# A hybrid decoder step on one Trainium2 core: the places of the gate products in the RWKV recurrence

## The chip, the core and the metric

The kernel runs on one core of one Trainium2 chip. The metric is the device time of one execution in microseconds (us). The core has a matrix engine (TensorE, PE in the rows; its weight loads are PEld), VectorE (DVE), ScalarE (ACT), GpSimd (POOL) and SyncE (SP), which here issues most DMAs. The engines run their own instruction streams and meet by semaphores.

## What is computed

One decoder layer is applied to 256 prompt tokens and 32 sample tokens (8 sequences of 4). Cut to what matters here:

```
P  = rmsnorm(x) @ w_in                    # 1024 -> HGRN2 | RWKV-7 | gate_a, gate_b (2 x 1024 columns)
o_a = hgrn2_chunked(...)                  # branch A
S   = S*diag(w) - (S kk)(kk*a)^T + v k^T  # branch B, RWKV-7, token by token
y   = S r ;  o_b = groupnorm(y)*... * g
merged = sigmoid(gate_a) * (o_a @ w_branch_a) + sigmoid(gate_b) * (o_b @ w_branch_b)
x = x + merged @ w_out
x = x + moe_top4of32(rmsnorm(x)) ; final rmsnorm
```

The 2048 gate columns are wanted only when the branches are merged. They depend on nothing of the recurrence.

## The kernel before

**The recurrence in passes.** RWKV-7 on the prompt is done in chunks of 32 tokens. The loop `for u in range(4)` at L872 makes four passes; a pass handles 128 tokens (four chunks) of four heads. In a pass TensorE works through small products in a fixed order, which VectorE and ScalarE answer from PSUM:

- `chunk_scores` and `scores` (L896, L905), then `level(0)` (L941, L944), the first of five levels that invert the 32x32 triangular parts by repeated squaring;
- `to_rows(At, Bn)` (transposes, L924), site L0, `level(1)`;
- `to_rows(Kn, vR)`, site L1, `level(2)`;
- `key_scores` (L912), site L2, then the key product Y1 (L980). It waits for the third rise of `rw_T_evac`, which ScalarE makes when it has copied the key rows (`knT`, L1733) after the two copies of level 2 (`power_evac(2)`);
- `level(3)`, site L3, `level(4)`, site L4, `solve` (L957), the sums of the earlier pass's output (L869), site W, the products L993 to L1005, the second sums, site Y;
- the chunk products (L1016 to L1020) with a site after each head, k0 to k3. VectorE turns their result into `phi`, one operation for each chunk (L2240). From the second pass on, four transposes (L1029) follow k3;
- the chain over the four chunks: L1040 and L1049, then a site (c0 to c3). Chunk c's L1040 waits for `phi` of chunk c and for the state that VectorE made of chunk c-1 (L2248).

**The sites.** At a site `fill(u, site)` (L669) issues so many gate products: one is a matmul of a 128x128 weight block with 288 token columns in float32, which the trace shows as two MATMUL records (L660). Eight products sum one block of 128 gate columns in one of two PSUM banks; there are 16 blocks. The first 56 products stand before the passes, 18 stand in each pass. How many stand at a site is the table `FILL` (L378), written by hand:

```python
FILL = (("L0", 1), ("L1", 1), ("L2", 1), ("L3", 1), ("L4", 2), ("W", 2), ("Y", 2), ("k0", 0), ("k1", 0), ("k2", 0), ("k3", 1),
        ("c0", 2), ("c1", 1), ("c2", 1), ("c3", 3))
```

`gate_products` (L383) sums the table up to a site. ScalarE's `gate_evacs` (L1686) reads the same sum: at a site at which it passes a multiple of eight, ScalarE takes the finished block out of PSUM by an Exp (L1606). Site W of ScalarE's stream stands before `ob_square`, whose result the second sums (L869) need; in the first pass two DMA issues (L1636) stand before it too.

After the passes come the branch products (L1072), the merge, `w_out` (L1098), the router, and the experts (L1304, L1325 and others). The experts' weights stream from HBM into eleven places, each refilled when TensorE has used it.

Of the kernel before, what the change touches and what calls it, by code (L numbers as in the profile page):

```python
# [76 lines left out]
def layer_kernel(nc, x_prompt, x_sample, state_hgrn, state_rwkv, state_shift, norm1_w, w_in, hgrn_lb_logits,  # L77
# [5 lines left out]
    with ctx:  # L83
# [288 lines left out]
        def pj_after(n):  # L372
# [2 lines left out]

        E_BLOCK = 31
        WHOLE = 7
        FILL = (("L0", 1), ("L1", 1), ("L2", 1), ("L3", 1), ("L4", 2), ("W", 2), ("Y", 2), ("k0", 0), ("k1", 0), ("k2", 0), ("k3", 1),  # L378
                ("c0", 2), ("c1", 1), ("c2", 1), ("c3", 3))
        GATED = (0, 2, 1)  # L380
        FILL_U = sum(n for _, n in FILL)

        def gate_products(u, site):  # L383

            x = [name for name, _ in FILL].index(site)
            return KT * WHOLE + u * FILL_U + sum(n for _, n in FILL[:x + 1])

# [2291 lines left out]
```

How the kernel before makes its waits and increments, by code:

```python
        def done_wait(eng, ins, name):  # L257
            eng.wait_ge(S(name), done(ins, name))
# [12 lines left out]
        def half_wait(turn, s):  # L272
            if turn is None and (s == SPLIT or s - FULL in HALVED):
                nc.tensor.wait_ge(S("half_loaded"), 16 * (1 if s == SPLIT else HALVED.index(s - FULL) + 2))
# [55 lines left out]
        def pe_w_wait(turn, s):  # L331
            if turn is None:
                nc.tensor.wait_ge(w_loaded[place(s)], 16 * loads_into(place(s), s + 1))
            else:
                n = PEELED + s
                per_turn = QUAD * ECH // WS
                nc.tensor.wait_ge(w_loaded[place(n)], turn * (16 * per_turn) + 16 * (loads_into(place(n), n + 1) - TURN * per_turn))
# [56 lines left out]
        @block.sync  # L395
        def _(sp):
            sp.dma_start(norm_bc[0:1, :], norm1_w).then_inc(S("norm_loaded"), 16)
            for t, (o, n) in enumerate(TILES):
                src = x_prompt[0, o:o + n, :] if t < 2 else x_sample.rearrange("b t d -> (b t) d")
                sp.dma_start(xs[0:n, t, :], src).then_inc(S(f"x_loaded{t}"), 16)
            sp.dma_start(xn[NS:NS + NB, 2, :], state_shift[0]).then_inc(S("shift_loaded"), 16)
            for n in list(range(N_IN + 2)) + [N_IN + 6, N_IN + 7] + list(range(N_IN + 2, N_IN + 6)):
                if N_IN - 1 <= n < N_IN + 3:
                    sp.wait_ge(S("rw_W"), 2 * (n - N_IN + 2))
                if n == N_IN + 6:
                    sp.wait_ge(S("rws_out"), 16 * NB)
                if n == N_IN + 4:
```

## Time and profile before

| | us |
|---|---|
| median of 3 runs | 1298.42 |
| the runs | 1297.34 to 1302.24 |
| the profiled execution | 1299.21 |
| its span, first to last instruction | 1297.5 |
| TensorE busy | 1264.7 (97%) |
| the four passes, in the span | 206.3 to 311.4 |
| the experts' stage, in the span | about 392 to the end |

Times of rows are from the start of the span. Matmuls overlap in the array and their ends are modelled, so what a group of them costs is read from its start to the start of the next group. A semaphore's wait shows as the idle time in brackets at the end of a row only where nothing modelled covers it; the distance of two starts shows it always.

### The profile page before, as it was taken

The numbers are of one execution on the slowest core, as the hardware profiler recorded it, in microseconds if no ns is written. First come the engines' busy times: TensorE is split into PE (matmuls) and PEld (weight loads), VectorE is DVE, ScalarE is ACT, GpSimd is POOL, SyncE is SP. The second block draws the span as 40 slices with busy tenths as digits, with TensorE's granted clock in tenths as the row PEclk, the third lists the DMA queues.
The fourth block names the chain that finished last, engine by engine and source line by source line (L and its number), as shares of the span: only waits on it lengthen the run. The fifth ranks groups of instructions, "written<-read, shape, count | busy, mean of one in ns | idle before, by whom it ended". The sixth has DMA issues, their size and how long they took to land.

```text
span 1297.5 us, 20685 instructions
## 1 busy us (share of the span) xinstructions
PE 1264.7 (97%) x8541; PEld 588.6 (45%) x8541; DVE 362.1 (28%) x1012; ACT 239.4 (18%) x544; POOL 55.1 (4%) x120
## 2 busy tenths in 40 slices
PE   8999999999999999999999999999999999999997
PEld 6768767777653333333333333333333323233333
DVE  2334766443346112112121121112121111211112
ACT  3144343232032011101111111011110101110102
POOL 5000300000060000000000000000000000000000
PEclk9999999999999999999999999999999999999999
DMA  7645424423989999999999999999999999999996
GB/s 221 163 130 194 131 67 129 144 101 117 372 297 377 426 429 429 428 428 428 429 429 429 428 429 430 430 429 429 430 431 430 429 430 429 430 430 430 429 429 260
DMA packets 73261, 449.55 MB, mean 346 GB/s; under 512 B 14408, under 2 KB 43130, under 8 KB 47884
## 3 DMA queue, kind: packets, MB, share of 16 engines
q1 hardware_dynamic: 67462, 445.45, 84.1%
q10 hardware_dynamic: 5734, 3.14, 0.9%
q8 instruction: 51, 0.84, 0.3%
q14 instruction: 14, 0.11, 0.0%
HBM read 443.82 MB, written 4.76 MB: 346 GB/s over the span
## 4 chain that ended last, share of the span: by engine, by line
PE 78%; DMA 16%; DVE 3%; ACT 2%; issue 1%; ACTq 0%; SPq 0%; DVEq 0%
PE bank L1304 26%; PE bank L1325 14%; DMA arena<-in_expert_w_gu_dram 7%; DMA ring<-in_expert_w_gu_dram 7%; PE bank L570 7%; PE bank L1219 5%; PE bank L660 5%; PE bank L1250 5%; PE bank L1072 2%; ACT arena L1449 2%; PE bank L1226 1%; PE bank L1294 1%; DMA arena<-in_norm_w_dram 1%; PE bank L617 1%; PE bank L1315 1%; PE bank L941 1%
## 5 line engine op out<-in xcount | busy, mean ns | idle before, releaser
L1304 PE MATMUL bank<-ring,arena 128*64 128x512 f32 x1040 | 233.6, 594 | 5.0 <-DMA ring<-in_expert_w_gu_dram 5.0
L1449 ACT ACTIVATE arena<-bank 128x512 f32<-128x512 f32 (+6 forms) x237 | 117.5, 511 | 451.5 <-PE bank L1325 196.2
L1304 PE MATMUL bank<-arena 128*64 128x512 f32 x768 | 173.3, 594 | 2.4 <-DMA arena<-in_expert_w_gu_dram 2.4
L1449 ACT ACTIVATE arena<-arena 128x256 f32<-128x256 f32 (+7 forms) x124 | 68.8, 564 | 471.9 <-DVE arena L2430 463.6
L1304 PEld LDWEIGHTS bank<-ring,arena 128*64 128x64 f32 x1040 | 72.8, 137 | 146.3 <-issue 122.6
L2430 DVE TENSOR_SCALAR arena<-bank 128x256 f32<-128x256 f32 x64 | 26.9, 421 | 377.6 <-PE bank L1304 377.6
L1325 PE MATMUL bank<-ring,arena 128*64 128x512 f32 x544 | 121.9, 595 | 0.0
L2476 DVE COPY arena<-bank 64x512 f32<-64x512 f32 x30 | 20.8, 694 | 316.6 <-PE bank L1325 316.6
L1304 PEld LDWEIGHTS bank<-arena 128*64 128x64 f32 x768 | 53.9, 137 | 105.8 <-issue 92.6
L1219 PE MATMUL bank<-arena 128*64 128x512 f32 x372 | 89.6, 599 | 0.0
L570 PE MATMUL bank<-arena,ring 128*128 128x296 f32 (+1 forms) x352 | 88.9, 415 | 0.0
L1325 PE MATMUL bank<-arena 128*64 128x512 f32 x352 | 79.8, 596 | 0.0
L570 PEld LDWEIGHTS bank<-arena,ring 128*128 128x128 f32 x352 | 67.7, 193 | 20.4 <-issue 0.8
L660 PE MATMUL bank<-arena,ring 128*128 128x288 f32 x256 | 76.8, 423 | 0.0
L1325 PEld LDWEIGHTS bank<-ring,arena 128*64 128x64 f32 x544 | 37.8, 137 | 70.6 <-issue 69.2
L1250 PE MATMUL bank<-arena 128*32 128x256 f32 (+1 forms) x252 | 66.3, 491 | 0.0
L1304 PE MATMUL bank<-extra,arena 128*64 128x512 f32 x240 | 54.2, 593 | 0.7 <-DMA extra<-in_expert_w_gu_dram 0.7
L1219 PEld LDWEIGHTS bank<-arena 128*64 128x64 f32 x372 | 23.8, 134 | 60.6 <-issue 60.6
L660 PEld LDWEIGHTS bank<-arena,ring 128*128 128x128 f32 x256 | 44.0, 189 | 12.0 <-issue 2.9
L1449 ACT ACTIVATE ring<-bank 128x128 f32<-128x128 f32 (+8 forms) x102 | 27.4, 311 | 100.0 <-PE bank L570 50.4
L1325 PEld LDWEIGHTS bank<-arena 128*64 128x64 f32 x352 | 24.3, 137 | 45.2 <-issue 45.0
L1250 PEld LDWEIGHTS bank<-arena 128*32 128x32 f32 (+1 forms) x252 | 24.8, 148 | 34.4 <-issue 34.4
(378 smaller groups left out, 1058.8 us busy)
## 6 DMA issues: line engine op xcount, KB each, us to landing
ring<-in_expert_w_gu_dram SPq DMA_DIRECT2D x63, 2048.0 KB, 24.0
arena<-in_expert_w_gu_dram SPq DMA_DIRECT2D x47, 2048.0 KB, 23.1
ring<-in_expert_w_down_dram SPq DMA_DIRECT2D x35, 2048.0 KB, 23.7
arena<-in_expert_w_down_dram SPq DMA_DIRECT2D x21, 2048.0 KB, 25.1
extra<-in_expert_w_gu_dram SPq DMA_DIRECT2D x15, 2048.0 KB, 25.8
ring<-in_w_in_dram SPq DMA_DIRECT2D x23, 1024.0 KB, 5.4
extra<-in_expert_w_down_dram SPq DMA_DIRECT2D x6, 2048.0 KB, 26.3
ring<-in_w_out_dram SPq DMA_DIRECT2D x4, 1024.0 KB, 8.6
```

The costliest lines, as they stand in the source:

```text
L570: i = mm(b[:, 0:cols], slot[:, kt, j * P:(j + 1) * P], xv[:, kt, 0:cols], start=(kt == 0), stop=(kt == KT - 1))
L617: i = mm(bank[k % 4][:, 0:CPC], xv[:, kt, P * t:P * (t + 1)], slot[:, kt, :], start=(kt == 0), stop=(kt == KT - 1))
L660: i = mm(bank[g % 2][:, 0:NT], slot[:, kt, (g % 2) * P:(g % 2 + 1) * P], xv[:, kt, 0:NT], start=(kt == 0), stop=(kt == KT - 1))
L941: i = mm(pair[rr, b + lo:b + hi], PTQ[rr, a + 2 * C:a + 3 * C], PTQ[rr, a + lo:a + hi], start=True, stop=True)
L1072: i = mm(bank[n % 2][:, 0:NT], slot[:, kt % 2, j * P:(j + 1) * P], (obT if br else oaT)[:, kt * NT:(kt + 1) * NT], start=(kt == 0), stop=( ...
L1219: i = mm(bank[6][64 * h:64 * h + 64, :], sel[0:rows, t * SLOTS:(t + 1) * SLOTS], x2[0:rows, t, h * 512:(h + 1) * 512], start=(t == 0), sto ...
L1250: return mm(out, GT[:, o:o + rows], yo[:, c], start=False, stop=True, skip_group_check=True)
L1304: ins = mm(bank[q % 2][64 * (q // 2):64 * (q // 2) + 64, :], gu_lhs(c), w[:, q * 512:(q + 1) * 512], start=(c == 0), stop=(c == KT - 1), s ...
L1325: ins = mm(b[64 * h:64 * h + 64, :], lhs(j, r), w[:, r * D + h * 512:r * D + (h + 1) * 512], start=(j == 0 and r == 0), stop=(j == DN - 1 ...
L1449: return nc.scalar.activation(out, in_, f, **kw)
L2430: v.tensor_scalar(by_row(glu, b), gu_half(b, 0), LIMIT, None, ALU.min).then_inc(S("glu_ready"), 1)
L2476: v.tensor_copy(yo[64 * x:64 * x + 64, 512:1024], bank[1][64:128, :]).then_inc(S("y_evac"), 1)
```

## The change

The counts of eight sites change; their sum stays at 18 for a pass. Sites L0, L1 and L3 go from one product to two, L2 and k3 from one to none, c0 from two to one. The order of all other instructions of TensorE stays, and so does their number. The places at which ScalarE takes finished blocks follow the table: in the first pass the block that was taken at W is taken at L4; in the second from L4 to L3; in the third from L3 to L1 and from c0 to Y; in the fourth from L1 to L0 and from Y to W.

```diff
-        FILL = (("L0", 1), ("L1", 1), ("L2", 1), ("L3", 1), ("L4", 2), ("W", 2), ("Y", 2), ("k0", 0), ("k1", 0), ("k2", 0), ("k3", 1),
-                ("c0", 2), ("c1", 1), ("c2", 1), ("c3", 3))
+        FILL = (("L0", 2), ("L1", 2), ("L2", 0), ("L3", 2), ("L4", 2), ("W", 2), ("Y", 2), ("k0", 0), ("k1", 0), ("k2", 0), ("k3", 0),
+                ("c0", 1), ("c1", 1), ("c2", 1), ("c3", 3))
```

## Rows read from the trace of the kernel before

**Rows 1.** The page: busy time of the engines and its weight loads' group (busy, mean ns).
```profile
PE 1264.7 (97%) x8541; PEld 588.6 (45%) x8541; DVE 362.1 (28%) x1012; ACT 239.4 (18%) x544; POOL 55.1 (4%) x120
L660 PEld LDWEIGHTS bank<-arena,ring 128*128 128x128 f32 x256 | 44.0, 189 | 12.0 <-issue 2.9
```
**Rows 2.** Windows: length, busy PE, PEld, DVE, ACT, POOL, clock, DMA share, GB/s.
```profile
258.60:284.75 26.15, 26.15 (x653) 19.87 (x652) 13.15 (x38) 8.37 (x21) 0.00 (x0) 1.00 0.33 123
...
392.00:1290.00 898.00, 881.50 (x4202) 308.37 (x4198) 181.04 (x585) 112.15 (x218) 0.00 (x0) 1.00 1.00 424
```
**Rows 3.** Waits of TensorE in the four passes: total us, times, longest.
```profile
PE bank L924 <- issue: 0.5, 1, 0.5
PE bank L869 <- ACT arena L1449: 0.2, 1, 0.2
```
**Rows 4.** Timeline of TensorE, third pass: start, us, line, shapes.
```profile
265.64 0.75 PE L660 MATMUL bank<-arena,ring 128*128 128x288 f32 x2
266.23 1.00 PE L980 MATMUL bank<-arena 128*128 128x64 f32 x8
...
267.95 0.75 PE L660 MATMUL bank<-arena,ring 128*128 128x288 f32 x2
268.64 0.46 PE L941 MATMUL bank<-ring 32*32 32x32 f32 x32
...
271.73 1.13 PE L660 MATMUL bank<-arena,ring 128*128 128x288 f32 x4
272.79 0.66 PE L993 MATMUL bank<-arena 128*64 128x128 f32 x8
```
**Rows 5.** Timeline of ScalarE, third pass, around the key product.
```profile
264.77 0.64 ACT L1449 ACTIVATE ring<-bank 128x128 f32<-128x128 f32 x2 [0.62 <-PE bank L944]
265.30 0.38 ACT L1449 ACTIVATE arena<-bank 128x256 f32<-128x256 f32 x1
```
**Rows 6.** Timeline of TensorE, third pass, from site k3 to the second chain step.
```profile
277.19 0.75 PE L660 MATMUL bank<-arena,ring 128*128 128x288 f32 x2
277.87 0.43 PE L1029 MATMUL bank<-arena,ring 32*128 32x32 f32 x4
278.23 0.45 PE L1040 MATMUL bank<-arena,ring 64*64 64x64 f32 x8
...
278.81 1.24 PE L660 MATMUL bank<-arena,ring 128*128 128x288 f32 x4
279.98 0.45 PE L1040 MATMUL bank<-arena,ring 64*64 64x64 f32 x8
```
**Rows 7.** Timeline of VectorE, third pass, phi and the first state.
```profile
277.58 1.26 DVE L2240 TENSOR_TENSOR ring<-bank,arena 128x128 f32<-128x128 f32 x4
278.88 0.29 DVE L2248 TENSOR_TENSOR arena<-bank,arena 128x128 f32<-128x128 f32 x1
```
**Rows 8.** Timeline of ScalarE, first pass, before the second sums.
```profile
221.77 0.41 ACT L1449 ACTIVATE arena<-bank 128x288 f32<-128x288 f32 x1 [1.94 <-PE bank L660]
222.07 0.30 ACT L1449 ACTIVATE arena<-arena 128x128 f32<-128x128 f32 x1
```
**Rows 9.** Timeline of TensorE, first pass: the second sums and the second chain step.
```profile
222.43 0.49 PE L869 MATMUL bank<-arena 128*128 128x128 f32 x2 [0.20 <-ACT arena L1449]
...
227.59 0.45 PE L1040 MATMUL bank<-arena,ring 64*64 64x64 f32 x8
```
**Rows 10.** Timeline of VectorE, first and last pass: the first state.
```profile
226.57 0.29 DVE L2248 TENSOR_TENSOR arena<-bank,arena 128x128 f32<-128x128 f32 x1
...
305.55 0.29 DVE L2248 TENSOR_TENSOR arena<-bank,arena 128x128 f32<-128x128 f32 x1
```
**Rows 11.** Timeline of TensorE, last pass: the second chain step.
```profile
306.73 0.45 PE L1040 MATMUL bank<-arena,ring 64*64 64x64 f32 x8
```
**Rows 12.** Groups of TensorE in 14 to 16.2 and in 24 to 30: count, busy, mean ns.
```profile
L570 PE MATMUL bank<-arena,ring 128*128 128x296 f32 x5 | 2.7, 701 | 0.0
...
L570 PE MATMUL bank<-arena,ring 128*128 128x296 f32 x25 | 6.4, 412 | 0.0
```
**Rows 13.** Window 12 to 16, columns as in rows 2.
```profile
12.00:16.00 4.00, 3.51 (x19) 2.72 (x18) 0.55 (x1) 1.41 (x4) 2.97 (x14) 0.69 0.68 199
```
**Rows 14.** Waits of TensorE from 400 us on, longest in total.
```profile
PE bank L1304 <- DMA ring<-in_expert_w_gu_dram: 5.0, 6, 1.2
```

## The prediction

> **What bounds the kernel now.** I read the page first: TensorE is busy 97% of the span and no other engine 30% [rows 1]. Then the windows, to see whether that holds where the change is: in the third pass TensorE is busy 26.15 of 26.15 us at a full clock, VectorE half of that, and the DMA engines a third [rows 2]. The waits of the four passes together show 0.7 us of TensorE's idle time, 0.2 of it on ScalarE and 0.5 on nothing that the profile names [rows 3]. So the passes are bound by TensorE's own stream. Since ends are modelled, the costs must be read from start to start; this is what the timelines are for. The experts' stage, two thirds of the span, holds both limits at once: DMA share 1.00 at 424 GB/s, TensorE 881.5 of 898 us busy [rows 2], its largest wait on weights 5.0 us in all [rows 14]. Its weights are let in by TensorE's own use of the eleven places, so I take a shift of the passes' end to be handed on in full.
>
> Nothing is added or removed. The total can only move by two small things: what it costs to go into and out of a group of gate products, and waits that a group had covered.
>
> **What a group costs.** One product between small steps takes 0.59 us at L2 (265.64 to 266.23) and 0.69 at L3 (267.95 to 268.64); two take 1.06 at W (271.73 to 272.79) [rows 4] and 1.17 at c0 (278.81 to 279.98) [rows 6]. A second product in a group adds 0.47 or 0.48. So a group has a cost of its own of 0.59 - 0.48 = 0.11 us behind wide tiles and 0.69 - 0.48 = 0.21 behind 32- or 64-row tiles.
>
> **Sites L0, L1, L3: one to two.** L0 and L1 follow 128-row transposes and cost 1.06 - 0.59 = 0.47 more each; L3 follows a level, 1.17 - 0.69 = 0.48. Together +1.42 a pass, +5.68 in four. The levels behind them had no wait to lose, so nothing is won by their longer cover.
>
> **Site L2: one to none.** The group's 0.59 goes. Key product Y1 waits for ScalarE's third copy. In the third pass TensorE is ready for Y1 at 265.64, where the removed group began [rows 4]; ScalarE's last copy runs 265.30 to 265.68 [rows 5]. How long after a copy's end TensorE starts is shown once: in the first pass the square ends at 222.07 + 0.30 = 222.37 [rows 8] and the sums that wait for it start at 222.43 [rows 9], 0.06 later. So Y1 starts at 265.74, 0.49 earlier instead of 0.59. The copies follow level 2, which stands just as far ahead as before. Four passes: -1.96. What is late next is level 3, which needs the copies of level 2, and these end by 264.77 + 0.64 = 265.41 [rows 5].
>
> **Sites k3 and c0: one to none, two to one.** These I take together, since VectorE works through them without a break. In the third pass k3 began at 277.19 and cost 0.68; the transposes take 277.87 to 278.23, 0.36; the first chain step starts at 278.23 [rows 6]. Without k3 TensorE would be ready for it at 277.19 + 0.36 = 277.55. But `phi` of chunk 0 is the first of four operations of VectorE from 277.58 [rows 7]; one takes 0.29 as the same shape below it, so it ends at 277.87 and the step can start at 277.93, 0.38 late. VectorE is not moved by the change here: `phi` stands behind its work on the earlier pass's output, which begins at ScalarE's answer to the second sums, well ahead of k3. The step takes 278.23 to 278.81, 0.58; c0 with one product behind a 64-row tile 0.69. That puts the second chain step at 279.20. The first state (L2248) stands on VectorE behind all four `phi` and ends at 278.88 + 0.29 = 279.17 [rows 7], so with 0.06 the step starts at 279.23. It was 279.98 [rows 6]: -0.75. By the state's end plus 0.06 the first pass gives 226.92 against 227.59, -0.67, and the last 305.90 against 306.73, -0.83 [rows 9 to 11]; the second lies as the last. Together -0.75 - 0.67 - 0.83 - 0.83 = -3.08, where without the waits it would be (0.68 + 0.48) x 4 = -4.64.
>
> **ScalarE's blocks.** In the first pass a gate block is taken at 221.77, between two DMA issues and the square of 222.07 [rows 8], and TensorE waits 0.20 for the square [rows 9]. The block goes to L4, so the square comes some 0.3 earlier: -0.20. In the fourth pass a block comes into the same place, but there no DMA issue stands ahead; the block's products end with W, three groups of eight products (L993 to L1005) before the second sums, and 0.41 for the block [rows 8] and about 0.4 for the square (a copy of its 256 columns takes 0.38 [rows 5]) should fit. I cost it at nothing; without that room it would cost the 0.20. The other moved blocks stand behind copies that they don't delay. PSUM banks and weight chunks: a block starts at most one group earlier, and TensorE shows no wait for a weight chunk or a bank in the passes [rows 3]; I cost this at nothing, and an unseen wait there would be one of the half microseconds below.
>
> **The sum.** 5.68 - 1.96 - 3.08 - 0.20 = +0.44 us. On the profiled execution's 1299.21 that is 1299.65; that execution was 0.79 above the median of the runs, 1298.42, so for the median I say 1298.9.
>
> **Bounds of what no row shows.** The trace has no TensorE wait at these places. From below, none of them costs anything: -4 x 0.59 at L2 and -4.64 give 5.68 - 2.36 - 4.64 - 0.20 = -1.52, or 1296.9. From above, each of the twelve waits (Y1, the first and the second chain step, four times) leaves one weight load in the open, 0.19 [rows 1], for it cannot be drawn ahead of the wait: +2.3, together +2.7, or 1301.1. I keep the middle since the one wait shown, 0.06 after the copy, had no such load on top. The 0.5 us of idle time without a cause [rows 3] may go or come twice.
>
> **A rule weighed against it.** The weight load of a gate product is 0.19 and a further product adds 0.48 for two MATMUL records [rows 1, 4], so within a group the loads are hidden behind matmuls in the same rows of the array. The Trainium skill, "TensorE: Matmul & The Clock Gate", section "The mechanism" of the part on packing small matmuls, says that a weight load overlaps running matmuls only when its row group differs. By that rule a longer group would save nothing, and this change would bring only its waits. The rows speak against it. As a mechanism of this kernel it is the fourth case below.
>
> **The rivals.**
> - *The covers still hold.* If VectorE and ScalarE finish earlier relative to TensorE than the rows say, no wait appears and the group costs are saved: -1.5, 1296.9. For it: both engines are half idle [rows 2]. Against: `phi` stood at the tail of an unbroken run of VectorE.
> - *Waits with their start-up.* 1301.1, above. For it: each wait also stops weights from being loaded ahead.
> - *The shift is absorbed.* The experts' weight stream, not TensorE, sets the end and takes up half a microsecond: 1298.4. For it DMA share 1.00; against it the stream's start hangs on TensorE.
> - *A group has no cost of its own.* A product costs 0.48 wherever it stands; then the moves are even and only waits remain: 4.64 - 3.08 + 4 x 0.10 - 0.20 = +1.8, 1300.2.
> - *Slower: the clock falls.* If the new waits at the chain bring TensorE's clock down for a pass, its matmuls grow as they did at the start, where after idle stretches the clock was 0.69 [rows 13] and a matmul of 296 columns took 701 ns against 412 at full clock [rows 12]. A pass of 26.15 us would take 26.15 x (701/412 - 1) = 18 more, 1316.8. It decides over 0.5% from about a third of a pass on. Against it: the waits are under 0.5 us each, no longer than the idle 0.5 that the passes already hold at a clock of 1.00.
> - *It does not do what it says*: the table is read by TensorE's and ScalarE's streams alike, so no mismatch can arise; no chance of its own.
>
> **How the numbers follow.** Forecast +0.4 (from -0.3 to +1.2): 45%. Covers hold 18%; start-up 17%; absorbed 8%; no group cost 10%; clock 2%. Predicted is the likeliest, 1298.9. The range goes from below the covers' case, by the half microsecond without a cause, 1296.4, to above the start-up case by the same and a part of the spread of the runs shown (1297.34 to 1302.24): 1302.3. About 0.5%, 6.5 us, is what a measurement can tell from no change: under 1291.9 none of the cases comes, I leave 2% for what I don't see; over 1304.9 the clock and the unseen, 3%; the same 95%.
>
> **What would show it.** In the trace after: a pass some 0.1 us longer; L980 0.06 after the end of ScalarE's third copy; the first chain step 0.06 after the end of the first L2240; c1's L1040 0.06 after L2248's end; no wait of L869 on ScalarE in the first pass and none in the fourth; the clock 1.00. Wrong would be: no delay at the chain (covers hold), a delay of 0.2 or more after the releaser's end (start-up), passes longer by 0.5 each, or an experts' stage that changes its own length by more than a microsecond.

## The result and the profile after

The changed kernel's median is 1300.39 us (1298.67 to 1304.67, 22 runs) against 1298.33 for the kernel before (1296.98 to 1302.73, 22 runs). The ratio is 1.0018, with a 95% interval of 1.0010 to 1.0027: slower by 2.1 us, beyond the interval but well inside the 0.5% (6.5 us) that the prediction called no change. The forecast was 1298.9 in 1296.4 to 1302.3. The range held and the sign was right; the size was not: 0.4 us were forecast. Some runs of every kernel are about 4 us longer than its others; the last section says why. In the text below a pass is one turn of the loop at L872, as before.

First the page and the windows of the four passes, with the columns of rows 2; the last window is a stretch behind the router that is taken up further down.

```profile
span 1302.9 us, 20685 instructions
...
PE 1267.9 (97%) x8541; PEld 590.7 (45%) x8541; DVE 360.2 (28%) x1012; ACT 239.3 (18%) x544; POOL 55.3 (4%) x120
```
```profile
204.94:232.74 27.80, 25.61 (x652) 19.39 (x649) 12.95 (x40) 10.26 (x33) 0.00 (x0) 1.00 0.42 126
232.74:259.69 26.95, 26.51 (x653) 20.09 (x652) 13.11 (x38) 8.68 (x21) 0.00 (x0) 1.00 0.32 120
259.69:286.43 26.74, 26.24 (x653) 19.99 (x652) 13.16 (x38) 8.37 (x21) 0.00 (x0) 1.00 0.32 121
286.43:313.45 27.02, 26.33 (x654) 20.19 (x654) 10.55 (x32) 6.38 (x19) 0.00 (x0) 1.00 0.13 42
385.00:396.00 11.00, 10.98 (x51) 7.05 (x50) 5.34 (x21) 2.90 (x8) 1.83 (x7) 0.53 0.67 254
```

The third pass took 26.15 us before [rows 2] and takes 26.74. The first took 26.02, from its first L896 to the next pass's, and takes 27.80; this is where most went. TensorE's waits in the passes name it; before, the second line of [rows 3] said 0.2:

```profile
PE bank L869 <- ACT arena L1449: 1.5, 1, 1.5
PE bank L1040 <- DVE ring L2240: 0.7, 2, 0.4
PE bank L924 <- issue: 0.7, 2, 0.5
PE bank L1040 <- issue: 0.3, 1, 0.3
```

**The first pass.** ScalarE's timeline after, and the second sums that wait for its square:

```profile
219.07 3.90 ACTq L1636 DMA_DIRECT2D out_dram<-ring  x2
223.02 0.31 ACT L1449 ACTIVATE arena<-arena 128x128 f32<-128x128 f32 x1 [3.57 <-issue]
```
```profile
223.38 0.49 PE L869 MATMUL bank<-arena 128*128 128x128 f32 x2 [1.53 <-ACT arena L1449]
```

The gate block that stood ahead of the square at 221.77 [rows 8] has gone to L4, as meant. Yet the square is later within its pass, since the two DMA issues (L1636) before it occupy ScalarE's queue for 3.90 us. Before they took 2.27, from the same view:

```profile
219.45 2.27 ACTq L1636 DMA_DIRECT2D out_dram<-ring  x2
```

What else is at that moment is in SyncE's timeline, first before, then after. The row is the load of the last weight chunk of the gates (chunk 22):

```profile
220.84 0.37 SPq L433 DMA_DIRECT2D ring<-in_w_in_dram  x1
```
```profile
219.06 0.37 SPq L433 DMA_DIRECT2D ring<-in_w_in_dram  x1
```

Before, the load was issued 1.4 us behind ScalarE's first issue (219.45). Now it is issued 0.01 ahead of it. The load waits for two things: a finished gate block, that is the eighth product of the first pass, and the first pass's `solve` (L957). The table moved the eighth product from site W, behind `solve`, to site L4, ahead of it. So `solve` is now what the load waits for last, as SyncE's waits from 216 to 220 us show:

```profile
SPq L433 <- PE bank L957: 1.0, 1, 1.0
```

`solve` also releases ScalarE's copy at 219.07, and behind that copy stands the first store issue. This is why the load and the issue start in the same moment. The experiments show that the moment of the load is the cause of the longer issues.

**The third pass, key product.** TensorE and ScalarE after:

```profile
267.02 0.72 PE L912 MATMUL bank<-arena 64*128 64x128 f32 x8
267.77 1.11 PE L980 MATMUL bank<-arena 128*128 128x64 f32 x8
```
```profile
267.34 0.38 ACT L1449 ACTIVATE arena<-bank 128x256 f32<-128x256 f32 x1
```

The copy ends at 267.72 and Y1 starts at 267.77, 0.05 later; 0.06 was forecast. From the key scores to Y1 it is 0.75 us.

**The third pass, chain.** TensorE and VectorE after:

```profile
279.95 0.45 PE L1040 MATMUL bank<-arena,ring 64*64 64x64 f32 x8 [0.31 <-DVE ring L2240]
...
280.54 0.75 PE L660 MATMUL bank<-arena,ring 128*128 128x288 f32 x2
281.34 0.45 PE L1040 MATMUL bank<-arena,ring 64*64 64x64 f32 x8
```
```profile
279.61 1.27 DVE L2240 TENSOR_TENSOR ring<-bank,arena 128x128 f32<-128x128 f32 x4
280.91 0.29 DVE L2248 TENSOR_TENSOR arena<-bank,arena 128x128 f32<-128x128 f32 x1
```

The first `phi` ends at 279.61 + 0.29 = 279.90 and the first step starts at 279.95, 0.05 later; 0.06 was forecast. The first state ends at 281.20 and the second step starts at 281.34, 0.14 later where 0.06 was forecast.

### The profile page after: what moved, and what is told of

It reads as the page before. It is cut to its first block, busy times and chain, and to the rows that moved or that the text cites. A ratio compares the mean times of both kernels' runs of the same rounds, so it can differ in the third digit from the quotient of the medians.

```text
span 1302.9 us, 20685 instructions
## 1 busy us (share of the span) xinstructions
PE 1267.9 (97%) x8541; PEld 590.7 (45%) x8541; DVE 360.2 (28%) x1012; ACT 239.3 (18%) x544; POOL 55.3 (4%) x120
## 4 chain that ended last, share of the span: by engine, by line
PE 79%; DMA 15%; DVE 3%; ACT 2%; issue 1%; ACTq 0%; SPq 0%; DVEq 0%
PE bank L1304 26%; PE bank L1325 13%; DMA arena<-in_expert_w_gu_dram 7%; DMA ring<-in_expert_w_gu_dram 7%; PE bank L570 7%; PE bank L1219 5%; PE bank L660 5%; PE bank L1250 5%; PE bank L1098 2%; PE bank L1072 2%; ACT arena L1449 2%; PE bank L1226 1%; PE bank L1294 1%; PE bank L617 1%; PE bank L1315 1%; PE bank L941 1%
## 5 line engine op out<-in xcount | busy, mean ns | idle before, releaser
L1304 PEld LDWEIGHTS bank<-arena 128*64 128x64 f32 x768 | 53.9, 137 | 105.8 <-issue 92.6
```

Of the source, the lines that this page charges most:

```text
L1304: ins = mm(bank[q % 2][64 * (q // 2):64 * (q // 2) + 64, :], gu_lhs(c), w[:, q * 512:(q + 1) * 512], start=(c == 0), stop=(c == KT - 1), s ...
```

## The experiments

Every median stands beside that of the kernel before on the same chip. The kernels of experiments 1 to 4 share one chip and one set of those runs (1297.99), those of experiments 5 to 7 another (1298.19). Intervals are 95%. Waits are those of TensorE in the four passes; the view leaves out anything under 0.15 us.

**1. Site L2 alone** (from the kernel before; the counts of `FILL` that change, before and after).

```diff
- L2 1, L3 1
+ L2 0, L3 2
```


> Edit: the kernel before with L2 one to none and L3 one to two, all else as before. Theory A (a new wait costs only the 0.06 us after its releaser): per pass -0.49 for L2 and +0.48 for L3, so 0.0 us a pass and 0.0 in all. Theory B (a new wait also leaves a weight load in the open, as the trace after hints, where the group of Y1 takes 1.03 us from start to start against 0.93): +0.1 a pass, +0.4 in all, and Y1's group at 1.03 again. A rival by which L2's emptying is what costs most of the 2 us: +1.5 or more.

Median 1298.28 us against 1297.99, ratio 1.0007 (0.9990 to 1.0023). TensorE's waits in its passes:

```profile
PE bank L941 <- issue: 0.7, 2, 0.5
PE bank L924 <- issue: 0.4, 2, 0.2
PE bank L869 <- ACT arena L1449: 0.2, 1, 0.2
```

By the medians L2's part costs 0.3 us, between A and B; an interval of this width does not exclude the rival's 1.5. The waits do, for none of them is the changed kernel's large one. Y1's group is at 1.03, as B said. ScalarE's two issues take 2.29 us, and the square's wait is 0.2, as before: here the eighth product stays at W.

**2. The chain alone** (from the kernel before; again the counts that change).

```diff
- L0 1, L1 1, k3 1, c0 2
+ L0 2, L1 2, k3 0, c0 1
```


> Edit: the kernel before with k3 one to none, c0 two to one, L0 and L1 one to two; L2 and L3 stay at one. Theory A: +0.94 for L0 and L1, -0.75 for k3 and c0 in the third pass, so +0.2 a pass, +0.8 in all. Theory B (start-up behind each of two waits): +0.3 to +0.35 a pass, +1.3 in all, with 0.74 us from the transposes' start to the first chain step in passes two to four and 0.81 from c0's product to the second chain step. Whoever holds that the whole loss comes from the chain expects +2.0.

Median 1299.41 against 1297.99, ratio 1.0014 (0.9996 to 1.0031). Waits:

```profile
PE bank L869 <- ACT arena L1449: 1.4, 1, 1.4
PE bank L1040 <- DVE ring L2240: 0.7, 2, 0.4
PE bank L1040 <- issue: 0.4, 2, 0.2
```

In this kernel the eighth product is at L4 (2 + 2 + 1 + 1 + 2), and the first pass's wait is there with its whole 1.4 us, though nobody expected it of this edit. So L2 has no part in it, and about half of what this edit costs is not the chain's own: from start to start L0 and L1 add 3.9 us in four passes, the chain gives back 2.7, and the wait adds 1.2. From the transposes to the first step it is 0.74 us and from c0's product to the second step 0.81, as B said.

**3. The store issues later** (from the changed kernel).

```diff
                 done(fn(yaT[:, 256:512], bank[4][:, 0:256], ACT.Copy), "rw_W_evac")
-                if u == 0:
-                    for g in range(2):
-                        sample_states_out(g)
...
                 if u < 3:
                     gate_sigmoid(u)
+                if u == 0:
+                    for g in range(2):
+                        sample_states_out(g)
```


> Edit: the changed kernel with ScalarE's two DMA issues of the sample states (L1636) moved in the first pass from ahead of the square to behind the gate's sigmoid. Theory C (the first pass's 1.5 us wait of the second sums on the square comes from the second issue, which occupied ScalarE's queue for 3.4 us against 1.8 in the trace before, and not from where the gate products stand): the wait is gone, the first pass is 26.2 to 26.5 us instead of 27.8, and the median is 0.3 to 1.5 us below the changed kernel's. Rival D (the square is late for another reason, such as the block taken at L4): the wait stays and the time too.

Median 1299.84 against 1297.99, ratio 1.0012 (0.9995 to 1.0029); the changed kernel beside it had 1299.94. The mechanism came out as C said: the square is no longer waited for and the first pass is 26.24 us. The gain did not come. The second pass took 28.43 us, with this wait at its first level:

```profile
PE bank L941 <- issue: 1.6, 1, 1.6
PE bank L1040 <- DVE ring L2240: 0.7, 2, 0.4
```

The time was handed back as a wait on nothing that the profile names. It is taken up in experiment 8.

**4. The changed kernel again.**

> Edit: none, the changed kernel once more beside the others, with a second look at its trace. Theory C expects the second issue to take between 1.8 and 3.4 us again, with the wait going with it, and passes two to four at 26.4 to 26.7 us. If the clock's stretch at 1.2 GHz between 385 and 396 us belongs to the change, it stands there again; if it falls where it happens to, the trace may show none or another and the end then moves by 3 us without the passes moving.

Median 1299.94 against 1297.99, ratio 1.0011 (0.9997 to 1.0025). The second issue took 3.47 us and the wait is 1.6: both belong to this kernel. The passes together took 107.5 us, against 108.5 in the first trace. This second trace shows no wait on "issue" of 0.15 us or more in its passes.

**5. The load held back** (from the changed kernel).

```diff
+                if n == N_IN - 1:
+                    sp.wait_ge(S("rw_R"), 1)
                 if n == N_IN:
```


> Edit: the changed kernel, with one more wait on SyncE: the load of the last weight chunk of the gates (chunk 22) also waits for the first pass's L999 products, so that it is issued about when it was in the kernel before, behind ScalarE's two issues. Theory E (the change lets the block of L4 finish earlier, this frees the chunk's place earlier, the load is issued at the same moment as ScalarE's first issue, and the two queues' packets get in each other's way, so that the second issue holds ScalarE for 3.4 us): the second issue takes 1.8 to 1.9 us again, the wait of the first pass's second sums falls from 1.5 to 0 to 0.3 us, the first pass is 26.3 us, and the median is 1.2 to 1.5 us below the changed kernel's, near 1298.6. Rival (the issue is long because the block taken at L4 moved, with no part of the load): 3.4 us again and no gain.

The timelines of SyncE and ScalarE (its lines stand two further down):

```profile
220.86 0.37 SPq L435 DMA_DIRECT2D ring<-in_w_in_dram  x1
```
```profile
218.44 2.29 ACTq L1638 DMA_DIRECT2D out_dram<-ring  x2
220.77 0.31 ACT L1451 ACTIVATE arena<-arena 128x128 f32<-128x128 f32 x1 [1.96 <-issue]
```

Holding the load back alone brings the issues back to 2.29 us and takes the wait away; the first pass is 25.95 us. Theory E holds for the cause: when the load is issued decides how long ScalarE's issues last. How it does so is not shown: in experiment 3 the second issue took 2.97 us though the load had landed, at 224.27, before that issue began at 224.55. The median was 1302.47 against 1298.19, ratio 1.0014 (0.9998 to 1.0030), and shows no gain. Two things hide one: the second pass has a wait on "issue" of 1.0 us at the same level as in experiment 3, and eight of these twelve runs hold a stretch at half clock behind the passes, which the last section explains. The four runs without it have a median of 1297.86, 0.5 us above such runs of the kernel before (1297.33, 22 runs). For the changed kernel of experiment 4 this difference is 1.8 (1299.58, 9 runs, against 1297.74, 24 runs). Four runs are few, but they speak for about the 1.2 to 1.5 us that E expected.

**6. The key rows early** (from experiment 5's kernel).

```diff
-                gate_evacs(u, "L1")
-                power_evac(2)
-                done(fn(knT, bank[2][:, 0:256], ACT.Copy), "rw_T_evac")
+                done(fn(knT, bank[2][:, 0:256], ACT.Copy), "rw_T_evac")
+                gate_evacs(u, "L1")
+                power_evac(2)
```


> Edit: as after_load_held, and ScalarE copies the key rows (knT) right behind the value rows, ahead of the two copies of level 2, so that Y1 has nothing to wait for though L2 is empty. Theory B (a wait costs its length and about 0.1 us of a weight load that cannot be drawn ahead of it): L912's group 0.65 us instead of 0.75 and Y1's 0.93 instead of 1.03, together -0.2 a pass, -0.8 in all against after_load_held. Theory A (only the wait's 0.06 to 0.1 counts): -0.1 a pass, -0.4 in all.

Median 1298.33 against 1298.19, ratio 1.0002 (0.9986 to 1.0017). An edit worth some 0.4 us does not show in it. TensorE in the third pass:

```profile
264.92 0.71 PE L914 MATMUL bank<-arena 64*128 64x128 f32 x8
265.56 1.10 PE L982 MATMUL bank<-arena 128*128 128x64 f32 x8
```

The key scores' group is back at 0.64: the wait cost 0.10. But Y1's group stays at 1.03 from start to start against 0.93 before (266.23 to the next level at 267.16), with no wait at all. So B's reason was wrong. The 0.10 belongs to Y1 standing straight behind small products with no gate product ahead of it. The "group's own cost" of 0.11 at L2 was never to be saved: 0.10 of it came back in Y1.

**7. VectorE's order too, and the same order with the old table.** The first kernel is experiment 6's with this, given in outline; the second is the kernel before with the new orders of both engines, its table and its load as before.

```diff
-                ob_final(u)
-                for c in range(4):
-                    phi of chunk c
+                for c in range(3):
+                    phi of chunk c
                 for c in range(4):
                     state of chunk c
+                    if c == 0:
+                        phi of chunk 3
+                    if c < 3:
+                        part c of ob_final(u)
```


> Edit: as after_held_key, and on VectorE phi of chunks 0 to 2 comes ahead of the earlier pass's output, whose three parts and phi of chunk 3 stand in the gaps of the chain. If the chain's wait is VectorE's order and nothing else, the first chain step starts 0.36 us behind the transposes' start or less than 0.55, c0's product takes 0.68 instead of 0.81, and a pass is 0.4 to 0.6 us shorter than in after_held_key; in all about 25.9 us a pass, and the time 1.5 to 2.5 us below the kernel before, near 1296. If the parts of the output delay the states in the gaps, the later chain steps grow from 1.27 us and the gain is lost.

> Edit: the kernel before, its table unchanged, with ScalarE's and VectorE's new orders of after_held_key and after_held_both. Its groups of gate products already cover these waits, so no gain: passes at 26.1 us, the median within 0.5 us of the kernel before. Against it after_held_both then shows what the two removed groups themselves are worth: 0.1 to 0.2 us each by the rows, 0.3 a pass, 1.2 to 1.5 in all. If a group has no cost of its own, the two are equal.

With the changed table: median 1297.47 against 1298.19, ratio 0.9989 (0.9973 to 1.0004). With the old table: 1297.53 against 1298.19, ratio 0.9985 (0.9969 to 1.0001). Both intervals reach one; neither kernel is shown to be faster than the kernel before, and they do not differ from each other. In the new order c0's product and the step after it are at 0.68 us and the first step at 0.47 to 0.59 from the transposes, so VectorE's order was the chain's wait, as forecast. But the third pass is not shorter with the changed table; first with it, then with the old one:

```profile
257.48:284.75 27.27, 26.33 (x654) 20.07 (x653) 13.17 (x38) 8.36 (x21) 0.00 (x0) 1.00 0.31 118
```
```profile
260.54:286.57 26.03, 26.03 (x654) 19.76 (x653) 13.16 (x38) 8.37 (x21) 0.00 (x0) 1.00 0.33 124
```

And the waits of the four passes with the changed table:

```profile
PE bank L1042 <- issue: 1.1, 2, 0.5
PE bank L943 <- issue: 0.5, 1, 0.5
PE bank L1042 <- DVE ring L2246: 0.4, 1, 0.4
PE bank L946 <- issue: 0.4, 1, 0.4
```

With the waits on engines nearly gone, 2.0 us of waits on "issue" stand in their place. The table in the next section takes them out; without them the passes of the two kernels are equal within 0.2 us.

**8. The code shifted** (from the changed kernel).

```diff
-            keep_busy(2, bank[5])
+            keep_busy(18, bank[5])
```


> Edit: the changed kernel with 16 more of the idle-time matmuls at its start (L580, 2 to 18), which is 64 more records of TensorE ahead of everything; the passes are untouched. Theory F (TensorE's waits on nothing that the profile names stand where its next piece of code, 16,384 bytes, has not come yet): they move 64 records towards the start of the passes, from the records 5247 and 7017 (counted without the added ones) to about 5183 and 6953, so from the last chain step of pass two to one before it and from the second transposes of pass four to level 1 or before. Rival (they belong to the operation, a semaphore or a bank): they stay at the same lines. The start gets about 1.8 us longer; the wait of the first pass on ScalarE stays at 1.4 to 1.6 us.

One run: 1301.68 us, of which the passes take 106.7 (108.5 and 107.5 in the two traces of the changed kernel); they begin 3.0 us later, not 1.8. All waits of its passes:

```profile
PE bank L869 <- ACT arena L1449: 1.5, 1, 1.5
PE bank L1040 <- DVE ring L2240: 0.7, 2, 0.4
```

The two waits on engines are there and none on "issue" is. That alone says little, for the changed kernel's second trace (experiment 4) shows none either. What decides is where these waits stand, and when.

Where: counted in TensorE's load and matmul records, the places in all the traces are 2973, 3225, 3477, 4237, 5247, 6007, 6511 and 7017. The distances are 252, 252, 760, 1010, 760, 504 and 506, multiples of about 253. The page's row of an instruction queue (packets, MB) gives the size of one fetch of code, 0.84 MB / 51 = 16 KB:

```profile
q8 instruction: 51, 0.84, 0.3%
```

The Trainium skill, "TensorE: Matmul & The Clock Gate", section "Step-by-step: what each phase is for", gives a matmul instruction 64 bytes; by that, an estimate, 16 KB are 256 instructions, and the 253 records agree.

When: the packets of queue q8 are in the traces with their times. All 36 waits of TensorE on "issue" in the passes of the thirteen traces end 1.2 to 1.6 us after the landing of such a packet. Each record always has the same packet, 2973 the 11th and 7017 the 27th, which is again 253 records for one packet. So these waits are late code; no operation and no semaphore accounts for them.

The shift agrees. F had the waits move by 64 records, to the operations that then stand at the same counts. In the shifted kernel nearly every 253rd record comes 1.6 us or more behind its packet, late enough to find its code there. The exceptions are 3477 and 5753 (two steps of 253 behind 5247), counted with the added ones, at 1.27 and 1.22 us. Near them TensorE is late by 0.1 and 0.2: level 1 of the third pass takes 1.00 us from start to start, and 0.83 in the twelve other traces. So two small moved delays are seen, and none at the old operations. Why the code comes later in one run than in another stays open.

**9. The kernel before, twice more.**

> Edit: none, the kernel before once more, for its trace. If the stretch of 10 us at half clock near 385 us, seen in both traces of the changed kernel, is chance, it may stand here too, and then the stretch from the router's transposes to the experts' first product is 3 us longer and the time about 1301 to 1302; the passes take 105 to 106 us and the second store issue 1.8 to 1.9 us either way. If it belongs to the change, it never stands here.

> As before_look_1, a third look at the kernel before. The longer stretch of passes of 105 to 106 us and an issue of 1.8 to 1.9 us are expected again.

1302.73 and 1301.59 us in single runs, against 1297.41 for another run of the kernel before on that chip. The passes took 106.3 and 105.8 us (105.1 in the first trace) and the second issue 1.83 and 1.85. Both hold the stretch at half clock; it is not the change's.

## Why the prediction was right and wrong

**What bounds the passes** was read rightly in the small and not in full. TensorE's stream sets the passes' length; but it also shares them with the arrival of its own code, which no busy share shows. The one row that pointed there, 0.5 us on "issue" [rows 3], I took for something that comes and goes without a cause. From start to start the same trace holds 1.6 us of it, most of it too short in each place for the view of waits.

A group of a given kind takes the same time, to about 0.02 us, in every pass and trace in which nothing holds it up. So the delays at every 253rd record can be summed from the starts and taken out of the passes. What is left is the same to 0.1 us in all traces of one kernel:

| kernel | the four passes, us | late code | passes without it |
|---|---|---|---|
| before, three traces | 105.07, 106.31, 105.83 | 1.63, 2.87, 2.38 | 103.44, 103.44, 103.45 |
| changed, two traces | 108.50, 107.52 | 2.14, 1.09 | 106.36, 106.43 |
| 1. L2 alone | 106.47 | 2.67 | 103.80 |
| 2. chain alone | 107.69 | 1.86 | 105.83 |
| 3. issues later | 108.19 | 3.44 | 104.75 |
| 5. load held back | 107.03 | 2.26 | 104.77 |
| 6. and key rows early | 106.29 | 1.95 | 104.34 |
| 7. and VectorE's order | 106.61 | 3.34 | 103.27 |
| 7. old table, new orders | 105.60 | 2.14 | 103.46 |
| 8. shifted | 106.68 | 0.48 | 106.20 |

The change costs the passes 2.9 us by this; in the medians it costs 2.1. That fits less late code in its traces than in those of the kernel before, 1.6 us on average against 2.3, though two and three traces are few. The 2.9 are taken back step by step: the load 1.6, the key rows 0.4, VectorE's order 1.1. Alone, L2's part costs 0.4, as B of experiment 1 said, and the chain's part 2.4, of which 1.2 is the wait for the square.

**L0, L1, L3** were costed at 0.47, 0.47 and 0.48 and measured 0.49, 0.48 and 0.49 in the third pass; in all 5.8 us against 5.7. Right.

**L2** was costed at -0.49 and measured -0.48 up to Y1's start (1.23 us from the key scores before, 0.75 after), and then +0.10 in Y1's own group; in all -1.5 against -2.0. What failed is the reading of the 0.11 as the group's own cost: nearly all of it had been a service to what stands behind it.

**k3 and c0** were costed at -0.75 in the third pass and measured 1.04 to 0.74 (-0.30) and 1.17 to 0.81 (-0.36), together -0.66. In all four passes it is -2.7 against a forecast -3.1. The mechanism, VectorE's four `phi` behind the earlier pass's output and then the state, was right: the first step came 0.74 us behind the transposes' start, as forecast. The second start-up was mis-sized, 0.14 against 0.06. Experiment 7 shows the cause directly by moving VectorE's work.

**Waits on "issue".** The third pass also holds a late third chain step, 0.90 us to its gate product instead of 0.58, at record 6511, which none of the kernels with the old k3 and c0 shows there; at record 6007 it lacks the 0.11 that the trace before has. With the terms above (+1.46 - 0.38 - 0.66) this gives the pass's +0.6 against a forecast +0.2. I had allowed for such waits only in the range.

**ScalarE's blocks** are the term that failed most: forecast -0.20, measured 1.5 - 0.2 = +1.3, the larger part of the 2.1 us. The prediction costed weight chunks at nothing, since TensorE shows no wait for one; it asked only whether TensorE would wait. It didn't ask what an earlier load meets. It meets ScalarE's stores, whose issue then holds ScalarE's stream, in which the square stands. Experiments 1, 2 and 5 separate this: the wait follows the place of the eighth product and the load's moment, not L2, and not the block's Exp.

**The moved block of the fourth pass** cost nothing, as forecast; no wait of L869 shows there.

**The range** held in part by luck. All four terms were forecast too low, by 0.2, 0.4, 0.4 and 1.5 us, which together makes +2.9 out of +0.4. The medians show only 2.1 of it, and the upper bound of 1302.3 had been set for another case, the start-up, with no such term for ScalarE in it.

**The rivals.** "A group has no cost of its own" came nearest in time (1300.2), though its sum has no +1.3 for ScalarE, so the time is luck. Its mechanism came nearer than its 10%: with the waits removed by order, the two tables give the same time (experiment 7) and the same passes without late code, 103.27 and 103.46 (0.3 of the second is the square's wait, which the held load takes away). "Waits with their start-up" (1301.1) was a little right: the second chain step has 0.08 more, but no delay reaches the 0.2 us that the prediction named as its sign, and Y1 and the first step have none more. "The covers still hold" fell at once. The clock did fall, but neither in the passes nor because of the change. "Absorbed" fell too: from the first L1260, just ahead of the experts' stage, to the end all thirteen traces take 907.3 to 908.6 us, 907.7 before and 907.8 in the first trace after, though it starts 5.4 us later there. What the passes lose is lost to the end. What experiment 5 gained in its first pass (1.7 to 1.9 us) it lost in part in its second (0.7 to 1.0).

## What to carry to other kernels

When a table moves work between sites, follow every semaphore that the moved work raises to the queue that listens, and ask what the earlier DMA will run into; a DMA issue stands in an engine's stream like any operation and can be held up there. Price a filler from start to start on both sides, since it also serves the operation behind it. When all named waits of a bound engine have been removed and the time stays, look at its waits on "issue", set them beside the packets of the instruction queue, and take them out before judging the schedule.

## What the runs showed of the hardware that was not expected

**A DMA issue's length can depend on another queue.** The second store issue (16x128 rows of 512 bytes) held ScalarE's queue for 1.82 to 1.86 us in the eight traces in which SyncE's 1 MB load was issued behind both store issues' starts, and for 3.28 to 3.47 us in the four in which the load was issued within 0.02 us of the first. In experiment 3, with the issues moved 5 us back, it was 2.97, though the load's data had landed 0.28 us before it began. So the load is one thing that lengthens an issue and not the only one; what the issue waits for is not shown.

**Late code.** TensorE waited up to 1.6 us on nothing named at records that lie about 253 apart or multiples of it, and went on 1.2 to 1.6 us after a 16 KB packet of its instruction queue had landed. In the passes these packets start no less than 3.3 us apart. Passes that gain a microsecond elsewhere can arrive at such a place earlier and wait there, as in experiments 3 and 5: late code took 1.1 to 3.4 us of the passes, and 0.5 in the shifted kernel.

**A stretch at half clock behind the router.** In six of thirteen traces, of both tables, TensorE's granted clock is 0.5, 1.2 GHz, for 10.2 us from 382 to 385 us on. Just before it TensorE runs the router's small products, and almost without a break: in the 10 us before the fall in experiment 9's first trace it is busy for 9.87 us, and its only wait from 366 us on is one of 0.5. The kernel before at full clock has a longer wait there, 0.8. So what makes the clock fall in one run and not in another is not shown. The windows from the first L1107 to the first L1260, in the first trace before and in experiment 9's first:

```profile
369.12:389.75 20.63, 19.66 (x140) 12.30 (x139) 10.29 (x38) 6.98 (x19) 10.13 (x13) 1.00 0.77 278
```
```profile
368.16:392.66 24.50, 23.84 (x139) 14.85 (x139) 10.98 (x39) 6.97 (x18) 10.37 (x13) 0.80 0.70 259
```

It costs 3.9 us here. Over all thirteen traces these windows take 19.8 to 20.6 us without the stretch and 23.3 to 24.5 with it. The first traces of the two kernels differ by 5.4 us in span: 3.4 are this stretch (24.01 against 20.63) and have nothing to do with the change, 3.4 are the passes, and 1.4 were gained before the passes began. A comparison of two single traces would have blamed the change for all of it. The stretch shows in a run's mean granted clock, which is 0.994 or 0.995 in the six traced runs that hold it and 0.997 to 0.999 in the seven others. It is also why medians of twelve runs, as in experiment 5, can lie 4 us from where their kernel's other runs are. Among runs of 0.998 or more, the changed kernel (experiment 4) is 1.8 us above the kernel before, L2 alone 0.4, the chain alone 1.1, the issues later 1.9, the load held back 0.5, with the key rows 0.9, and the two kernels of experiment 7 stand at 0.0.
